# Another order for the branch phase: where modulation pieces, norm sums, a value tile and GpSimd's sums stand

## What is computed

```python
z = h @ W_in                                   # h = RMSNorm(s) * (1 + scale1) + shift1
g = sigmoid(z[..., OFF_GATE:]).reshape(B, T, 3, D_MODEL)
a = rwkv_output(...) @ rwkv_out                # branch A, y from the scans
b = silu(layer_norm(conv(u) + dw_b)) @ conv_out           # branch B, 512 channels
c = (u * (W_s @ layer_norm(v) + b_s)) @ sgu_out           # branch C, 512 channels, 128-token chunks
m = a * g[:, :, 0] + b * g[:, :, 1] + c * g[:, :, 2]
s += gate1 * (m @ w_merge)
```

## Time and profile before

| | us |
|---|---|
| median of 3 runs | 4165.7 |
| lowest, highest | 4157.65, 4166.03 |
| the profiled execution | 4153.69 |
| its span | 4151.6 |

### The profile page before, as it was taken

The page is one execution under the profiler, slowest core; times in us unless marked ns, Lnnn a source line. Parts: engine busy times, 40 slices in busy tenths (PEclk is TensorE's granted clock), DMA queues, the critical chain, the costliest instruction groups (busy, mean ns, idle before and its releaser), DMA issues.

```text
span 4151.6 us, 111541 instructions
## 1 busy us (share of the span) xinstructions
PE 3931.3 (95%) x51440; PEld 2573.0 (62%) x51440; DVE 1622.4 (39%) x2677; ACT 1141.2 (27%) x2005; POOL 426.1 (10%) x340
## 2 busy tenths in 40 slices
PE   7999999999987999999999989999998988999999
PEld 3566666666544555655545656666665445678887
DVE  3656666654941111322210255655554411132211
ACT  3444444442021000200000244544443211020100
POOL 0000000000022221122200000000000022314410
PEclk9999999999999999999999999999999999999999
DMA  5000000000431323211123400000010342242245
GB/s 201 25 8 24 24 24 24 29 27 26 160 121 47 95 82 93 82 55 61 61 76 102 145 25 9 23 23 23 23 33 28 129 168 63 84 142 90 90 132 155
DMA packets 80943, 294.16 MB, mean 71 GB/s; under 512 B 9184, under 2 KB 13536, under 8 KB 80096
## 3 DMA queue, kind: packets, MB, share of 16 engines
q1 hardware_dynamic: 72576, 252.74, 19.3%
q10 hardware_dynamic: 6624, 29.04, 1.8%
q0 software_dynamic: 1280, 5.24, 0.3%
HBM read 273.36 MB, written 13.63 MB: 69 GB/s over the span
## 4 chain that ended last, share of the span: by engine, by line
PE 89%; ACT 4%; issue 2%; DVE 2%; DMA 2%; POOL 1%; ACTq 0%; SPq 0%; DVEq 0%; POOLq 0%
PE psum L1078 16%; PE psum L1525 15%; PE psum L1481 12%; PE psum L962 11%; PE psum L697 11%; PE psum L1389 9%; PE psum L974 5%; PE psum L1110 2%; PE psum L688 2%; PE psum L922 2%; DMA ring<-w_stream_in 2%; PE psum L940 1%; PE psum L846 1%; ACT arena L1888 1%; ACT L1556 0%
## 5 line engine op out<-in xcount | busy, mean ns | idle before, releaser
L1078 PEld LDWEIGHTS psum<-arena 32*32 32x32 f32 (+3 forms) x40512 | 695.5, 117 | 357.7 <-issue 282.7
L1078 PE MATMUL psum<-arena 32*32 32x32 f32 (+4 forms) x40512 | 787.2, 207 | 87.2 <-issue 54.6
L962 PE MATMUL psum<-arena,ring 128*128 128x512 f32 (+1 forms) x1408 | 572.4, 523 | 5.4 <-issue 2.9
L1481 PE MATMUL psum<-arena,ring 128*128 128x256 f32 (+1 forms) x1920 | 518.1, 432 | 0.0
L697 PE MATMUL psum<-arena,ring 128*128 128x512 f32 (+1 forms) x1264 | 472.9, 532 | 33.5 <-DVE arena L2534 24.1
L1481 PEld LDWEIGHTS psum<-arena,ring 128*128 128x128 f32 x1920 | 364.8, 190 | 153.5 <-issue 116.2
L697 PEld LDWEIGHTS psum<-arena,ring 128*128 128x128 f32 x1264 | 241.9, 193 | 265.3 <-issue 208.0
L1525 PE MATMUL psum<-arena 128*128 128x384 f32 (+1 forms) x1344 | 368.6, 432 | 0.0
L962 PEld LDWEIGHTS psum<-arena,ring 128*128 128x128 f32 x1408 | 239.3, 190 | 145.1 <-issue 118.7
L1525 PEld LDWEIGHTS psum<-arena 128*128 128x128 f32 x1344 | 255.4, 190 | 106.4
L1525 PE MATMUL psum<-arena,ring 128*128 128x384 f32 (+1 forms) x1008 | 278.5, 432 | 0.0
(11 more groups left out here) (153 smaller groups left out, 3760.7 us busy)
## 6 DMA issues: line engine op xcount, KB each, us to landing
ring<-w_stream_in SPq DMA_DIRECT2D x472, 512.0 KB, 3.7
x_spill<-arena ACTq DMA_DIRECT2D x2, 3072.0 KB, 8.7
arena<-x_spill ACTq DMA_DIRECT2D x16, 384.0 KB, 6.6
arena<-ya_spill ACTq DMA_DIRECT2D x6, 768.0 KB, 6.1
ring<-w_stream_in ACTq DMA_DIRECT2D x8, 512.0 KB, 6.3
arena<-x_in ACTq DMA_DIRECT2D x1, 3072.0 KB, 14.1
arena<-ups_in SPq DMA_DIRECT2D x16, 192.0 KB, 2.4
ya_spill<-arena POOLq DMA_DIRECT2D x8, 384.0 KB, 7.1
```

Of the source, the lines that this page charges most:

```text
L962: mm = pe.matmul(bank(j, z=b - a), lhsT=w[k], rhs=hs[k][:, a:b], start=(k == 0), stop=(k == KT - 1))
L1078: return pe.matmul(out, lhsT=lhs, rhs=rhs, start=start, stop=stop, skip_group_check=True)
L1481: mm = pe.matmul(psum[:, tile, a - c0:b - c0], lhsT=w, rhs=mov[k][:, a:b], start=(k == 0), stop=(k == len(mov) - 1), skip_group_check=True)
```

## The change

`whole_flow` puts at most two modulation pieces at a place (before there were six behind svar and four behind G10); p00 moves from behind the spatial matmuls to between svar and the transposes; the turns of third 2 and of third 3 move later. cmean and cvar use tile 2 instead of tile 3, and p00, p01, p20 and p21 change tiles. On ScalarE G00's sigmoids come ahead of svar's root and the copies of the modulation move; on VectorE part p00 comes ahead of the spatial sums. GpSimd makes the sums for cvar ahead of G01's weights, and the weights of G11 behind the four merge sums of p20, p21, p10 and p11. `branch_flow` now ends before G10, and the body of the value tiles becomes a function `value_tile`. What is computed, and the number of matmuls, is the same.

```diff
@@ whole_flow, the order of the branch phase
     entry("smean")
     out.append(f"t{mod_thirds(l)[0]}")
-    out.extend(itertools.islice(mods, 2))
-    entry("G00")
-    entry("svar", 6)
+    for name in ("G00", "svar"):
+        entry(name)
+    entry("p00", 2)
     for j in range(CT):
         entry(f"tr{j}")
     for j in range(CT):
-        entry(f"sp{j}")
-    entry("p00", 2)
-    entry("G10", 4)
-    entry("p01")
-    out.append(f"t{mod_thirds(l)[1]}")
-    for name in ("cmean", "G20", "cvar", "G01", "p20", "p21", "p10", "p11"):
-        entry(name)
+        entry(f"sp{j}", 2 * (j == CT - 1))
+    for name, n in (("G10", 2), ("p01", 2), ("cmean", 0), ("G20", 2), ("cvar", 0), ("G01", 2), ("p20", 0), ("p21", 0), ("p10", 0), ("p11", 2)):
+        entry(name, n)
     for i in range(1, KT // 2):
         a, b = 2 * i, 2 * i + 1
         if i > 1:
             entry(f"G0{i}", 2)
-        else:
-            out.extend(itertools.islice(mods, 2))
         entry(f"p0{a}", 1)
+        if i == 1:
+            out.append(f"t{mod_thirds(l)[1]}")
         entry(f"G1{i}", 2)
         entry(f"p0{b}", 1)
+        if l == 0 and i == 3:
+            out.append("t3")
         entry(f"G2{i}", 2)
         for name in (f"p2{a}", f"p2{b}", f"p1{a}", f"p1{b}"):
             entry(name)
-        if l == 0 and i == 2:
-            out.append("t3")
@@ branch_tiles
-            at.update(p00=2, p01=2, p20=0, p21=2, p10=2, p11=0, cmean=3, cvar=3)
+            at.update(p00=0, p01=0, p20=2, p21=0, p10=2, p11=0, cmean=2, cvar=2)
@@ TensorE, merge_flow loop (cvar likewise, with take(tiles[name], A.at("cr")))
                     elif name == "cmean":
-                        take(3, None)
+                        take(tiles[name], V.at(f"cc{CT - 1}"))
                         pe.wait_ge(*G.at(f"ya{CT - 1}"))
@@ ScalarE, branch_phase
                 gate_copy("G00")
+                gate_sigmoids("G00")
                 act.wait_ge(*PE.at("svar"))
...
-                gate_sigmoids("G00")
                 gate_copy("G10")
                 gate_sigmoids("G10")
-                copied(mod_thirds(l)[1])
...
-                    elif name == "p15" and l == 0:
+                    elif name == "p11":
+                        copied(mod_thirds(l)[1])
+                    elif name == f"p0{KT - 2}" and l == 0:
                         copied(3)
@@ VectorE, branch_phase
+                part("p00")
                 for j in range(CT):
                     dve.wait_ge(*PE.at(f"sp{j}"))
...
-                part("p00")
                 gate_sums("G10")
                 part("p01")
-                mod_ready(mod_thirds(l)[1])
@@ GpSimd, branch_phase
                 gate_weights("G20")
+                summed("yq", lambda j: A.at(f"csq{j}"), CU[0], CU)
                 gate_weights("G01")
-                summed("yq", lambda j: A.at(f"csq{j}"), CU[0], CU)
...
-                for name in flow[flow.index("G01"):]:
-                    if name[0] == "G":
+                for name in flow[flow.index("G01") + 1:]:
+                    if name in added:
+                        merge_add(name)
+                    if name[0] == "G" or name == "p11":
                         following = next(upcoming, None)
                         if following:
                             gate_weights(following)
-                    elif name in added:
-                        merge_add(name)
```

More of the change, by code:

```diff
@@ L291, in branch_flow @@
     flow = whole_flow(l)
-    return flow[:flow.index("p00")]
+    return flow[:flow.index("G10")]
 def merge_flow(l):
     flow = whole_flow(l)
-    return flow[flow.index("p00"):]
+    return flow[flow.index("G10"):]
 def rows_of(pair):
@@ L331, in names_branch @@
     a = list(GELU_EARLY) + ["cb2", "cb3", "su3"] + [f"sv{j}" for j in range(CT)]
-    a += [f"ssq{j}" for j in range(CT)] + ["G00c", "sln", "sr"] + [f"sn{j}" for j in range(CT)] + [f"tr{j}" for j in range(CT)]
-    a += ["G00l", "G00h", "G00r"] + [f"G10{x}" for x in "clhr"] + [f"csq{j}" for j in range(CT)] + [f"G20{x}" for x in "clhr"]
+    a += [f"ssq{j}" for j in range(CT)] + [f"G00{x}" for x in "clhr"] + ["sln", "sr"] + [f"sn{j}" for j in range(CT)]
+    a += [f"tr{j}" for j in range(CT)] + [f"G10{x}" for x in "clhr"] + [f"csq{j}" for j in range(CT)] + [f"G20{x}" for x in "clhr"]
     a += ["cln", "cr", "G01c"] + [f"cs{j}" for j in range(CT)] + [f"G01{x}" for x in "lhr"]
@@ L343, in names_branch @@
             v += [f"y{j}_{n}"] + [x for x in SIDE[l].get((j, n), []) if x[:3] != "mod"]
-    v += [f"{x}{j}" for j in range(CT) for x in ("sp", "uv")]
-    v += ["p00"] + [f"G10{x}" for x in COMBINED] + ["p01"] + [f"cc{j}" for j in range(CT)] + [f"G20{x}" for x in COMBINED]
+    v += ["p00"] + [f"{x}{j}" for j in range(CT) for x in ("sp", "uv")]
+    v += [f"G10{x}" for x in COMBINED] + ["p01"] + [f"cc{j}" for j in range(CT)] + [f"G20{x}" for x in COMBINED]
     v += [f"G01{x}" for x in COMBINED[:4]] + [f"cn{j}" for j in range(CT)] + [f"G01{x}" for x in COMBINED[4:]]
@@ L349, in names_branch @@
     gates = [[f"{n}w{k}" for k in (1, 2, 3, 4)] for n in pairs_of_gates(l)]
-    g = SUMS[:3] + gates[0] + SUMS[3:6] + gates[1] + SUMS[6:9] + gates[2] + gates[3] + SUMS[9:]
+    g = SUMS[:3] + gates[0] + SUMS[3:6] + gates[1] + SUMS[6:9] + gates[2] + SUMS[9:] + gates[3]
     after = iter(gates[4:])
-    for n in merge_flow(l)[merge_flow(l).index("G01"):]:
-        if n[0] == "G":
+    for n in merge_flow(l)[merge_flow(l).index("G01") + 1:]:
+        if n[:2] in ("p1", "p2"):
+            g += [n.replace("p", "m")]
+        if n[0] == "G" or n == "p11":
             g += next(after, [])
-        elif n[:2] in ("p1", "p2"):
-            g += [n.replace("p", "m")]
     pe = list(GELU_EARLY)
@@ L1391, in gate_pair, with value_tile @@
                         mm.then_inc(*S.mark(f"{name}.{i}"))
+                def value_tile(name):
+                    tile, b, q = tiles[name], int(name[1]), name[2]
+                    own = f"p2{q}" if name[:2] == "p1" else name
+                    take(tile, V.at(name))
+                    if name == "p00":
+                        pe.wait_ge(s_back, 80 * (l + 1))
+                    if name == "p10":
+                        pe.wait_ge(*A.at(f"cs{CT - 1}"))
+                    if name == "p20":
+                        pe.wait_ge(*V.at(f"uv{CT - 1}"))
+                    arrived(pe, key, chunk[own])
+                    k0, nk = ((0, 8), (0, 4), (4, 4))[b]
+                    mov = (ya_, cv, sg)[b]
+                    project(pe, tile, chunk_blocks(chunk[own], k0, nk), mov, c0, c0).then_inc(*S.mark(name))
                 for name in branch_flow(l):
@@ L2014, in branch_phase @@
                 act.wait_ge(*PE.at("cvar"))
-                rsqrt(slot(NT, c0), psum[:, 3, 0:n], 1.0 / CONV, eps_c(1), "cln", "cr", A)
+                rsqrt(slot(NT, c0), psum[:, tiles["cvar"], 0:n], 1.0 / CONV, eps_c(1), "cln", "cr", A)
                 gate_copy("G01")
@@ L2603, in branch_phase @@
                     dve.tensor_tensor(slot(SU + j, c0), slot(SU + j, c0), slot(H1 + j, 0, n), ALU.mult).then_inc(*V.mark(f"uv{j}"))
-                part("p00")
                 gate_sums("G10")
                 part("p01")
-                mod_ready(mod_thirds(l)[1])
-                centred("cmean", 3, CY)
+                centred("cmean", tiles["cmean"], CY)
                 gate_sums("G20")
```

30 lines of the change are left out of this document (9 added, 21 removed).

## The result

| | before | changed |
|---|---|---|
| median | 4165.86 us (4 runs, 4157.65 to 4171.28) | 4104.83 us (4 runs, 4082.97 to 4105.83) |
| ratio, 95% interval | | 0.9843 [0.9806, 0.9879] |
| the profiled execution, its span | 4153.69, 4151.6 | 4105.65, 4103.6 |

The changed kernel is 61 us or 1.6% faster; forecast were 4098 us. One of its four executions took 4082.97 us, the other three 4104.01 to 4105.83. Run again for the experiments, on another chip, it had the same ratio: 0.9843 [0.9826, 0.986], 4100.81 against 4167.68 us.

What follows compares the result with a forecast made beforehand. TensorE, busy 3931 of 4151.6 us, bounds the kernel; only its idle and slowed time can be won. Gains of 35.5 and 35.0 us, less 3 for the clock, make 67.5: from the median 4165.7 to 4098 us, range 4078 to 4122.

Steps and rivals of the forecast that it cites:

- The sum: Both branch phases: layer 0 gains 35.5 us, layer 1 35.0, together 70.5; less 3 for the clock, 67.5.
- GpSimd's order in the merge: Before p02: merge sums ahead of G11's weights remove its wait (14.76 us in layer 0) and slow restart; G11 doesn't wait.
- One term: G11's weights after the last piece: chunks 3.6 and 1.2 us, two sums and start-up 2.7, in all 7.5 us.
- The covers: p02, a modulation piece, turn t2 and G11's first product hide G11's weights: 15 us in layer 0, 9.6 in layer 1.
- Norm sums: cvar's wait on GpSimd (most of 5.5 and 4.7 us) goes, as does cmean's 0.56 us wait.
- The walk round the ring: DMA waits left before G20 and G01: 1.1 us each in layer 0, 1.5 in layer 1; none at G00 or G10.
- VectorE in G00: G00's third product waits 2.2 us in layer 0 for VectorE, busy with taps; 0 in layer 1.
- The other waits: G10 waits 1.1 and 0.5 us for VectorE's last spatial sum; 0.3 us each between spatial matmuls.
- p00's cover: p00 between svar and transposes hides the chain svar, Ln, Exp, scaling; without it about 4.5 us of wait.
- The further drain: The skill's 1.38 us per table switch would add 2.7 us to ScalarE's chain; the prediction saw none in the trace.
- The clock: First parts of the branch phases: granted clock 0.97 or more instead of 0.91, with 3 us allowed for loss.
- The rival of the clock that falls as often as before: First parts stay at 0.91 clock, the 25 us there stay lost: 4120 us; chance 0.15.

Runs made afterwards that it cites:

- the second run: The changed kernel run again without an edit, on another chip: 4100.81 us against 4167.68 for the kernel before, ratio 0.9843.
- GpSimd's old order: The changed kernel with both GpSimd moves reversed (cvar's sums behind G01's weights, merge sums behind G11's): 4162.85 us, ratio 0.9992 to the kernel before.
- p00 back: The changed kernel with p00 behind the spatial matmuls again, two pieces behind svar and two behind p00: 4123.54 us, ratio 0.9903 to the kernel before.
- the tiles swapped: The changed kernel with the tiles of the transposes and spatial matmuls swapped: 4101.02 us, ratio 0.9842 to the kernel before.
- Three of them together: The changed kernel with G00's sums earlier on VectorE, single modulation pieces where the ring is tight, and transpose and spatial tiles swapped: 4084.21 us, ratio 0.9794.
- a fourth on top: Those three edits plus the merge's second-part branch-1 value tiles in PSUM tiles 1 and 2 instead of 2 and 1: 4084.84 us, ratio 0.9802.

## Why the prediction was right

**The sum.** Forecast were 35.5 + 35.0 us in the two phases, less 3 for the clock: 67.5. The profiles show 31.75 + 31.33 = 63.1, and 66.6 in the second run; the medians fell by 61.0 and 66.9. I had put the profiled execution's 12 us under the median down to executions. The short stretch with the scans, 6 to 16 us shorter than in every other profile, agrees with that.

**GpSimd's order in the merge.** The wait goes as foreseen: p02 starts at once and takes 10.59 us (7.13 in layer 1), and G11 waits for nothing. Priced alone it is 27.9 us. **One term was too small**: from the last piece to G11's second weight sum I reckoned 7.5 us, 3.6 + 1.2 of it for the chunks. It took 10.1 us in layer 0 (1306.5 to 1316.65) and 8.9 in layer 1 (3432.8 to 3441.70), since the two loads, behind a third, took 6.4 us from issue to landing. The covers were right, 15.0 and 9.5 us, so layer 1 had 0.6 us to spare where I said 2, and 1.1 in the second run. That no wait came out there is partly luck.

**Norm sums.** cvar has no wait. Price alone 9 us by the medians, 6.7 by the phases. What I didn't see is that the two halves of the change depend on each other: I said of the new flow only what it does to the ring, not that G01's chunks come later for GpSimd too. With the old order there cvar would have waited 14 us.

**The walk round the ring.** Right for G20 and G01 (forecast 1.1 in layer 0, found 1.09 and 1.16, the first of them put down to VectorE in this profile and to the DMA in the second, 1.22; forecast 1.5 with 1.0 for the second product, found 1.76 and 1.65 with 0.92 and 0.91). **Wrong for G00**: "its chunks are no longer behind m2.2 and m2.3, they land before it starts". The first does, the second takes the slot of sv3, freed just before, and lands in a train with others: waits of 0.73 and 1.84 us before G00, where none was forecast. The profile puts the 1.84 down to ScalarE; in the second run the same wait, 1.65, is put down to the DMA. The 0.8 us for GpSimd that I forecast at the second product of layer 1 is not there (0.16 in the second run). In layer 1 the slow restart adds 1.8 (3.75 us for 1.97).

**VectorE in G00.** Forecast 2.2 us, found 3.64 in both profiles of the changed kernel. The mechanism was right and the size off: I took over from the old trace how far VectorE was behind TensorE, its sum at 1165.64 being 14.8 us behind t1. In the changed kernel t1 starts at 1155.13 and the sum 17.8 us later:

```profile
1172.94 2.19 DVE L2539 TENSOR_TENSOR arena<-psum,arena 128x384 f32<-128x384 f32 x4
```

How far VectorE is behind TensorE there differs from profile to profile: its first sum starts 17.8 us behind t1 in the changed kernel run again too, but 14.4 in the kernels with GpSimd's old order and with p00 back, and 18.8 with the tiles swapped, whose programs are the same up to here. At 14.4 us product 3 of G00 waits 0.89 us, at 18.8 it waits 4.90. In the changed kernel VectorE's second sum was done 19.0 us behind t1 (15.9 forecast, 3.1 more), and TensorE came up to product 3 after 15.4 us (13.8 forecast, 1.6 more, of it 0.7 for the chunk). What sets VectorE's distance in an execution stays open.

**The other waits.** Before G10 1.42 and 1.33 (forecast 1.1 and 0.5), between spatial matmuls 1.13 once (0.3). Altogether TensorE idles 9.5 us in layer 0's first part from G00 on and 8.6 in layer 1's, against 5.8 and 6.7: 5.6 us more than forecast. TensorE is busy 94% and 92% there, not 96%.

**p00's cover.** "Without p00's cover about 4.5 us" was found at 4.93 in layer 1 (5.75 in layer 0). The two more table loads cost what the row said. ScalarE of the changed kernel:

```profile
1183.62 1.28 ACT L1555 ACT_TABLE_LOAD   x1
1184.91 0.90 ACT L1561 ACTIVATE arena<-psum,const 128x768 f32<-128x768 f32 x1
1185.84 1.28 ACT L1555 ACT_TABLE_LOAD   x1
1187.13 0.84 ACT L1564 ACTIVATE arena<-arena 128x768 f32<-128x768 f32 x1
```

Each function starts 1.29 us after its load began, and the second load starts 0.93 us after the Ln did, which runs 0.90. The further drain of 1.38 us for each switch of which the Trainium skill speaks (ScalarE: Activation LUTs, What ACT_TABLE_LOAD costs) is not to be seen here either.

**The clock.** Forecast 0.97 or more; found 0.98 and 0.97. The allowance was 3 us. By the rates of the second part (85.2 us for 256 records of the gates with 384 columns, 57.9 and 45.6 for 256 and 192 with 256 columns) the gates lost 45.5 - 42.6 in layer 0 and 29.9 - 28.9 and 24.8 - 22.8 in layer 1, together 5.9 us. Most of it is lost where TensorE restarts after the longer waits: 5.42 us for 2.74 after 3.64, and 3.75 for 1.97 after 1.84. The granted clock over G00's product 3 (the figure 0.51 or 1.00 in the row), in the changed kernel and then in the same kernel run again, where it took 2.85 us after the same wait:

```profile
1174.10:1179.50 5.40, 5.37 (x9) 2.97 (x10) 1.02 (x2) 0.00 (x0) 0.00 (x0) 0.51 0.00 0
```
```profile
1175.80:1181.00 5.20, 5.13 (x16) 3.15 (x17) 1.60 (x4) 0.52 (x1) 0.00 (x0) 1.00 0.00 0
```

After waits of 0.9 to 1.8 us before G10, G20 and G01 the products ran at full rate. The rival of the clock that falls as often as before, and with it the rule on short pauses (TensorE: Matmul & The Clock Gate, A second HAM failure mode, in the Trainium skill), didn't decide: seven waits of 0.9 to 1.4 us stand in the two first parts beside three of 1.6 to 1.9 and one of 3.64, and the granted clock was 0.98 and 0.97.

**The balance.** Waits 5.6 us over the forecast and gates 2.9 over the allowance make 8.5, but the phases fell short by 4.4 in the first profile, and by 0.9 in the second. Part of the difference is modulation, which took 8.5 us for 60 records in layer 0's first part where the rate of the earlier trace rows gives 10.1; the rest is not assigned. So the closeness of the time, 4104.83 us for 4098, is in part luck: misses of 8.5 us were half made up by something that I had not reckoned.

## What to carry to other kernels

A ring of buffers is read by counting back: chunk n can come when the user of n - 4 is done, so a cheap chunk put in the wrong place makes the next one wait for an expensive user, and one piece more or less at a place decides. An engine off the critical path (GpSimd at 10%) can hold both halves of such a loop, and then two edits are worth 37 and some 5 us alone and 67 together: test each by taking it out of the final kernel as well as by putting it alone into the old one. Edits of 1 to 9 us that no median shows one by one can be told by the wait that goes from the trace. Three of them together showed in the median, 17 us; a fourth on top did not.
